# Two transformer blocks on one core: the first feed-forward product and the entry into block two reordered on VectorE and ScalarE

## The reference, cut to what matters

```python
# end of the first block
x = x + m @ w_out
hf = rmsnorm(x, norm_ff_g)
z = relu(hf @ w_ff1)              # 1024 -> 4096
x = x + (z * z) @ w_ff2           # 4096 -> 1024
x = rmsnorm(x, norm_final_g)
# start of the second block
mod = silu(c) @ w_ada + b_ada     # 6 vectors of 1024
shift1, scale1, gate1, shift2, scale2, gate2 = split(mod, 6)
hn = rms_norm(x, g_norm1) * (1 + scale1) + shift1
proj = hn @ w_in                  # q_m k_m v_m o_m gates q_a k_a v_a
# ... mLSTM, attention, w_out, then
x = x + gate2 * hierarchical_moe(...)   # 32 experts, top 2 of one group
return rms_norm(x, g_final)
```

## Time and profile before

| | before |
|---|---|
| median of 3 runs | 1003.87 us (1002.82 to 1003.92) |
| the profiled execution | 1001.12 us |
| its span, first to last instruction | 999.2 us |
| TensorE busy | 971.4 us (97%) |
| VectorE busy | 566.9 us |
| ScalarE busy | 413.9 us |
| granted TensorE clock, mean | 0.997 |
| mean DMA rate | 329 GB/s |

### The profile page before, as it was taken

One profiled execution on the slowest core, in us unless ns is written; L12 is line 12 of the kernel. 1 busy time (PEld: TensorE's weight loads), 2 busy tenths in 40 slices (PEclk: granted clock), 3 DMA queues, 4 the chain that ended last, 5 costly groups with the idle time before them and its releaser, 6 DMA issues.

```text
span 999.2 us, 12464 instructions
## 1 busy us (share of the span) xinstructions
PE 971.4 (97%) x4936; PEld 635.6 (64%) x4936; DVE 566.9 (57%) x880; ACT 413.9 (41%) x647; POOL 83.8 (8%) x72
## 2 busy tenths in 40 slices
PE   8999999999999999989999999999999999899986
PEld 6888888887888888879988534343434343334432
DVE  5677767898989976776986522322323232223222
ACT  7734553445454444666685322222322222122223
POOL 0122003313322030010000000000000000000000
PEclk9999999999999999999999999999999999999999
DMA  9987559986777875545558999999999999999995
GB/s 329 391 306 259 178 170 360 325 292 217 279 255 279 314 270 189 198 159 197 178 198 332 381 417 423 428 429 440 424 439 426 429 433 436 426 425 427 425 424 234
DMA packets 73600, 328.35 MB, mean 329 GB/s; under 512 B 4812, under 2 KB 4976, under 8 KB 61120
## 3 DMA queue, kind: packets, MB, share of 16 engines
q1 hardware_dynamic: 71504, 323.68, 82.6%
q0 software_dynamic: 1888, 3.54, 1.4%
q10 hardware_dynamic: 144, 0.26, 0.1%
HBM read 326.39 MB, written 1.07 MB: 328 GB/s over the span
## 4 chain that ended last, share of the span: by engine, by line
PE 77%; DMA 9%; DVE 8%; ACT 3%; issue 2%; SPq 0%; DVEq 0%; ACTq 0%
PE bank L1095 19%; PE bank L1122 9%; DMA er<-in_w_experts 8%; PE bank L602 6%; PE bank L605 6%; PE bank L599 6%; PE bank L683 4%; PE bank L785 4%; PE bank L1064 3%; DVE wlo L1743 3%; PE bank L687 2%; PE bank L790 2%; PE bank L1134 2%; PE bank L659 2%; PE bank L656 2%
## 5 line engine op out<-in xcount | busy, mean ns | idle before, releaser
L1095 PE MATMUL bank<-er,XT 128*64 128x512 f32 x1024 | 236.1, 600 | 6.6 <-DMA er<-in_w_experts 6.3
L1743 DVE TENSOR_TENSOR wlo<-raw,whi 128x2048 fp32r<-128x2048 f32 x88 | 201.3, 2296 | 68.7 <-ACT whi L1208 68.7
L1208 ACT ACTIVATE whi<-raw 128x2048 fp32r<-128x2048 f32 x88 | 167.0, 1911 | 76.3 <-PE bank L605 33.0
L1095 PEld LDWEIGHTS bank<-er,XT 128*64 128x64 f32 x1024 | 70.4, 137 | 141.6 <-issue 133.7
L1122 PE MATMUL bank<-er,HT 128*64 128x512 f32 x496 | 112.3, 594 | 1.0 <-DMA er<-in_w_experts 1.0
L599 PE MATMUL bank<-whi,hh 128*128 128x512 f32 x224 | 87.9, 393 | 1.4 <-ACT whi L1215 1.4
L602 PE MATMUL bank<-wlo,hh 128*128 128x512 f32 x224 | 87.3, 390 | 0.2 <-DVE wlo L1752 0.2
L605 PE MATMUL bank<-whi,hl 128*128 128x512 f32 x224 | 87.3, 390 | 0.0
L1645 ACT ACTIVATE Y<-bank 64x512 fp32r<-64x512 f32 x62 | 36.6, 591 | 113.9 <-DVE bank L2446 113.1
L683 PE MATMUL bank<-f,whi 128*128 128x512 f32 x224 | 79.4, 399 | 0.0
L1122 PEld LDWEIGHTS bank<-er,HT 128*64 128x64 f32 x496 | 35.1, 137 | 68.4 <-issue 67.5
(11 more groups left out here) (385 smaller groups left out, 1578.1 us busy)
## 6 DMA issues: line engine op xcount, KB each, us to landing
er<-in_w_experts SPq DMA_DIRECT2D x27, 2048.0 KB, 39.4
er<-in_w_experts SPq DMA_DIRECT2D x49, 1024.0 KB, 9.2
er<-in_w_experts SPq DMA_DIRECT2D x12, 4096.0 KB, 34.4
raw<-in_w_in SPq DMA_DIRECT2D x41, 1024.0 KB, 6.2
er<-in_w_experts SPq DMA_DIRECT2D x8, 5120.0 KB, 28.7
raw<-in_w_ff SPq DMA_DIRECT2D x32, 1024.0 KB, 5.8
raw<-in_w_ada SPq DMA_DIRECT2D x24, 1024.0 KB, 5.8
raw<-in_w_out SPq DMA_DIRECT2D x8, 1024.0 KB, 7.3
```

The lines of the kernel that those rows point to most:

```text
L1095: m = e.matmul(b[64 * w:64 * w + 64, :], K.XT[:, j % 5, k, :], K.weights(i)[:, o:o + 512], start=k == 0, stop=k == 7)
L1208: e.activation(whi[K.ring(n)][:, :], raw[h.raw][:, :], ACT.Copy).then_inc(S["hi"], 1)
L1743: e.tensor_tensor(wlo[K.ring(n)][:, :], raw[h.raw][:, :], whi[K.ring(n)][:, :].bitcast(F32), ALU.subtract).then_inc(S["lo"], 1)
```

## The change

- `order_weights`: the `w_ada` half in unit 0 and the second one in unit 1 go; since the list ends after 24, two later ones appear, one in unit 6 and one in unit 7. The weights around them move up or down in the list by one or two places.
- First feed-forward product: VectorE does `x1_out(1)` before `lo(41)`, `f_lo(1)` and the sum of squares before `lo(42)`; ScalarE does `f_hi(1)` before `hi(42)`; TensorE does `turn_f(1)` after chunk 1, not 2.
- Entry: `xg` is split off from `x2_out` (`xg_out`) and, for the last quarter, done five steps later; the last quarter's x is moved ahead of the first `n_lo`; the squares change order with it; `n_lo(0, 7)` goes behind the factor of token block 1. `turn_x2(1, 1)` and `spread(1)` are now done inside token block 0, after chunks 3 and 6. Half 74 is passed on in pieces, the first high piece ahead of ScalarE's copy of the spread factor.
- Later: ScalarE does `hi(85)` before it copies the attention values, not after.

```diff
@@ -24,7 +24,7 @@
 RAW = 6
 RING = 3
 LATE = 96
-PIECED = (0, 1)
+PIECED = (0, 1, 74)
 FIRST2 = 72
 MSC = 128 ** -0.5
 ASC = 64 ** -0.5
@@ -313,10 +313,11 @@
             if g < 8:
                 cols(A["w_ff1"][0], 0, 512 * g)
                 cols(A["w_ff1"][0], 512, 512 * g)
-                ada()
+                if g > 0:
+                    ada()
             if g > 0:
                 rows(A["w_ff2"][0], 512 * (g - 1))
-                if g < 6:
+                if 1 < g < 6:
                     ada()
                 rows(A["w_ff2"][0], 512 * (g - 1) + 256)
         for c0 in (VM, QK, QK + 512, QA, KA, VA, OM):
@@ -614,7 +615,7 @@
             mid()
         dense_half(n + 1, xh, xl, 1, K.at[use], False, True, ready)
 
-    def dense_token(n, xh, xl, t, ready, mid):
+    def dense_token(n, xh, xl, t, ready, between=None):
 
         o = K.at["VM"][t][:, :]
         e.wait_ge(*K.before["VM"][t])
@@ -631,10 +632,10 @@
                 e.matmul(o, a_h, r_l, start=False, stop=False)
                 e.wait_ge(S["x_lo"], ready(k))
                 m = e.matmul(o, a_l, r_h, start=False, stop=k == 7)
-            if t:
-                m.then_inc(S["used"], 1)
-            if hf == 0:
-                mid()
+                if t and c == 3:
+                    m.then_inc(S["used"], 1)
+                if between:
+                    between(k)
 
     def dense_turned(use, n, xh, xl, ready=None, mid=None, each=None):
         free(use)
@@ -791,7 +792,7 @@
         return m
 
     dense_turned("ff0", 40, K.fh, K.fl, (lambda k: SPLIT["f"] + k + 1), None,
-                 lambda k: turn_f(1) if k == 2 else None)
+                 lambda k: turn_f(1) if k == 1 else None)
     for g in range(1, 8):
         dense_paired(f"ff{g}", 38 + 4 * g, K.f2)
         if g == 1:
@@ -825,9 +826,9 @@
 
 
     turn_x2(1, 0)
-    dense_token(72, K.nh, K.nl, 0, (lambda k: SPLIT["n"] + k + 1), lambda: turn_x2(1, 1))
-    spread(1)
-    dense_token(72, K.nh, K.nl, 1, (lambda k: SPLIT["n"] + k + 9), lambda: None)
+    dense_token(72, K.nh, K.nl, 0, (lambda k: SPLIT["n"] + k + 1),
+                lambda k: turn_x2(1, 1) if k == 3 else spread(1) if k == 6 else None)
+    dense_token(72, K.nh, K.nl, 1, (lambda k: SPLIT["n"] + k + 9))
     dense_turned("QK0", 74, K.nh, K.nl)
     free("gates")
     e.wait_ge(S["gw_s"], 4)
@@ -1369,10 +1370,8 @@
         e.wait_ge(S["x"], X_AT["1"] + t + 3)
         e.wait_ge(S["sq"], 5 + t)
         squares(K.x[:, t, 512:1024], 18 + t, K.vjunk[:, 512 * t:512 * t + 512])
+    f_hi(1)
     hi(42)
-
-
-    f_hi(1)
     root(3, 16)
     hi(43)
     for g in range(8):
@@ -1402,13 +1401,13 @@
     def x2_square(t, n):
         i = 2 * t + n
         e.wait_ge(S["x"], X_AT["2"] + i + 1)
-        e.wait_ge(S["sq"], 8 + 2 * i)
+        e.wait_ge(S["sq"], (8, 10, 12, 13)[i])
         squares(K.x[:, t, 512 * n:512 * n + 512], 24 + 4 * n + t, K.junk9[:, 512:1024], EPS ** 0.5 / 32)
 
     def xg_square(t, n):
         i = 2 * t + n
         e.wait_ge(S["xg"], i + 1)
-        e.wait_ge(S["sq"], 9 + 2 * i)
+        e.wait_ge(S["sq"], (9, 11, 14, 15)[i])
         squares(K.xg[:, t, 512 * n:512 * n + 512], 26 + 4 * n + t, K.junk9[:, 0:512], 1.0 / 32)
 
     def x2_root(t):
@@ -1436,18 +1435,20 @@
     x2_square(1, 0)
     e.wait_ge(S["l_col"], 64)
     n_hi(0, (0, 1))
+    x2_square(1, 1)
+    n_hi(0, (2, 3))
     xg_square(1, 0)
-    n_hi(0, (2, 3))
-    x2_square(1, 1)
     n_hi(0, (4,))
     xg_square(1, 1)
     n_hi(0, (5, 6, 7))
     x2_root(1)
+    hi_piece(74, 0)
     spread(1)
     n_hi(1, range(8))
-    hi(74)
+    for c in range(1, 4):
+        hi_piece(74, c)
+    hi(75)
     root(6, 24)
-    hi(75)
     e.wait_ge(S["turned"], TURNED["x2"] + 4)
     e.wait_ge(S["rs"], 6)
     for t in range(2):
@@ -1519,10 +1520,10 @@
             for t, o in ((0, slice(0, 128)), (1, slice(128, 384))):
                 e.activation(Sx[:, hq, o], Sx[:, hq, o], ACT.Exp, bias=stat(k + 4 * t + hq), scale=ASC,
                              accum_out=stat(k + 8 + 4 * t + hq)).then_inc(S["exp"], 1)
+    hi(85)
     e.wait_ge(S["used"], 84)
     for t in range(2):
         e.activation(K.vat[t][:, :], K.at["VA"][t][:, :], ACT.Copy).then_inc(S["vat"], 1)
-    hi(85)
 
     def flat(half):
         return K.PTt[half][:, :, :].rearrange("p h s -> p (h s)")
@@ -1936,16 +1937,16 @@
     x1_out(0)
     lo(40)
     f_lo(0)
+    x1_out(1)
     lo(41)
-    x1_out(1)
-    lo(42)
-
-
     f_lo(1)
     e.wait_ge(S["sq"], 8)
     e.tensor_tensor(stat(16, 2), stat(16, 2), stat(18, 2), ALU.add).then_inc(S["st"], 1)
     e.wait_ge(S["st"], ST_AT["1"] + 1)
-    inv_rms(3, 16, D)
+    e.tensor_scalar(stat(16, 2), stat(16, 2), 1.0 / D, EPS, ALU.mult, ALU.add).then_inc(S["ms"], 1)
+    lo(42)
+    e.wait_ge(S["sd"], 3)
+    e.reciprocal(stat(16, 2), stat(16, 2)).then_inc(S["rs"], 1)
     e.wait_ge(S["rs"], 3)
     e.tensor_tensor(stat(16, 2), stat(16, 2), stat(16, 2), ALU.mult).then_inc(S["st"], 1)
     e.wait_ge(S["l_late"], 16)
@@ -2001,11 +2002,14 @@
             e.wait_ge(S["used"], 72)
         e.scalar_tensor_tensor(out=K.x[:, t, o], in0=K.at["ffo"][i][:, :], scalar=stat(16 + t), in1=K.x[:, t, o],
                                op0=ALU.mult, op1=ALU.add).then_inc(S["x"], 1)
+
+    def xg_out(t, n):
+        o, i = slice(512 * n, 512 * n + 512), 2 * t + n
         e.wait_ge(S["x"], X_AT["2"] + i + 1)
         e.tensor_tensor(K.xg[:, t, o], K.x[:, t, o], K.nfb[:, o], ALU.mult).then_inc(S["xg"], 1)
 
     def x2_sums(t):
-        e.wait_ge(S["sq"], 10 + 4 * t)
+        e.wait_ge(S["sq"], 10 + 5 * t)
         e.scalar_tensor_tensor(out=stat(20 + t), in0=stat(24 + t), scalar=EPS * EPS, in1=stat(26 + t), op0=ALU.add,
                                op1=ALU.add).then_inc(S["st"], 1)
         e.wait_ge(S["st"], ST_AT["2"] + 1 + t)
@@ -2031,25 +2035,29 @@
         e.scalar_tensor_tensor(out=K.nl[:, q, o], in0=K.nf[:, q, o], scalar=K.ada_cols[:, q:q + 1],
                                in1=K.nh[:, q, o].bitcast(F32), op0=ALU.add, op1=ALU.subtract).then_inc(S["x_lo"], 1)
 
-    x2_out(0, 0)
-    x2_out(0, 1)
+    for n in range(2):
+        x2_out(0, n)
+        xg_out(0, n)
     x2_sums(0)
     x2_factor(0)
     x2_out(1, 0)
+    xg_out(1, 0)
     e.wait_ge(S["a1"], 2)
     e.wait_ge(S["ada_rows"], ROWS[10])
     e.wait_ge(S["Rb"], 1)
-    for q in range(3):
-        nf_out(0, q)
+    nf_out(0, 0)
+    nf_out(0, 1)
+    x2_out(1, 1)
     n_lo(0, 0)
-    x2_out(1, 1)
-    for q in range(1, 8):
-        if q < 6:
-            nf_out(0, q + 2)
-        n_lo(0, q)
+    for q in range(1, 7):
+        nf_out(0, q + 1)
+        if q == 3:
+            xg_out(1, 1)
         if q == 6:
             x2_sums(1)
+        n_lo(0, q)
     x2_factor(1)
+    n_lo(0, 7)
     e.wait_ge(S["Rb"], 2)
     nf_out(1, 0)
     nf_out(1, 1)
@@ -2057,10 +2065,11 @@
         if q < 6:
             nf_out(1, q + 2)
         n_lo(1, q)
+    for c in range(4):
+        lo_piece(74, c)
     e.tensor_tensor(stat(24, 2), stat(24, 2), stat(28, 2), ALU.add).then_inc(S["st"], 1)
     e.wait_ge(S["st"], ST_AT["2"] + 3)
     e.tensor_scalar(stat(24, 2), stat(24, 2), 1.0 / EPS, EPS, ALU.mult, ALU.add).then_inc(S["ms"], 1)
-    lo(74)
     e.wait_ge(S["sd"], 6)
     e.reciprocal(stat(24, 2), stat(24, 2)).then_inc(S["rs"], 1)
     for n in range(75, 79):
```

## The result

| | before | after |
|---|---|---|
| median, measured together | 1003.31 us (1002.75 to 1003.92, 6 executions) | 995.65 us (994.58 to 997.51, 6 executions) |
| ratio, 95% interval | | 0.993 (0.992 to 0.994) |
| the profiled execution | 1001.12 us | 997.51 us |
| its span | 999.2 us | 995.6 us |
| granted clock in it, mean | 0.997 | 0.994 |

The change makes the kernel 7.66 us faster. The forecast was 998.4 us with a range from 996.7 to 1001.2: the direction is right, the time lies 1 us under the range. Against 1003.87, the median that the forecast started from, 5.5 us were expected and 8.2 were found.

The account below looks back on a forecast made before the run. TensorE was taken as the bound to 560 us, then TensorE and DMA side by side. Terms 2.35 + 0.3 + 0.1 + 0.85 + 1.45 + 0.5 = 5.55, taken as 5.5, gave 998.4 us from 1003.87; range 996.7 to 1001.2.

Parts of the forecast that it names:

- First product and w_ada halves: First feed-forward product and units 0 and 1: 2.35 us from the new order, 0.3 us from moving the halves.
- the wait at line 687: Unit 1, TensorE waiting for lo(46) behind two w_ada halves: 0.3 us to be saved, 0 as the other end.
- line 656: Chunk 4 of the first feed-forward product: TensorE's 2.19 us wait for f_lo(1) goes, a term of 2.35 us.
- Entry: Entry to block two: token block 0 gives 0.1 us, the spread factor 0.85, half 74 1.45.
- The new wait on `nl`: Token block 0 at the entry: first n_lo begins later behind the last quarter's x, a new stall of 0.5 us.
- Half 74 in pieces: Entry, token block 1: low weights arrive piece by piece, so TensorE's stall at line 659 goes, saving 1.45 us.
- the rival in which the entry gives less back: Block 0 and the factor lose 2 us together, so the gain is 3.5 us: 1000.4 us; chance 0.14.
- OM product: Line 891: hi(85) ahead of the value copies starts 0.53 us earlier, saving 0.5 us, between 0 and 0.6.
- The stream moves: Expert weights from 560 us: DMA stream shifts with TensorE, adding or taking nothing; rival that it stays, 1003 us, chance 0.09.
- the moved sums cost nothing: Unit 7: last two partition sums on GpSimd end before the hand-over is needed, 6 us of cover, cost 0.
- the slower rival: Unit 7: both moved sums fall on the hand-over and hold VectorE, up to 9 us on TensorE: 1007.4 us; chance 0.05.
- The median stands 2.75 us above the profiled execution: Whole kernel: offset added to the forecast profiled execution of 995.6 us, giving a median of 998.4 us.

Follow-up runs that it names:

- only_entry: Kernel before with only the entry part of the change; weight order, first product and hi(85) as before: 1000.72 us, ratio 0.9974.
- busy_first: Kernel before with two unused 128x512 matmuls filling TensorE's stall at line 656: 1002.55 us, ratio 0.9997.
- busy_all: Kernel before with unused matmuls filling the stalls at line 656, before token block 1 and at line 659: 1002.44 us, ratio 0.9997.
- only_first: Kernel before with only the new order of the first feed-forward product, w_ada halves left in place: 1004.48 us, ratio 1.0013.
- only_ada: Kernel before with only the w_ada halves moved, order of the first product as before: 1002.48 us, ratio 0.9991.
- idle7: New kernel with TensorE nearly still at the start of units 1 to 7, eight tiny matmuls waited for one by one: 1030.67 us, ratio 1.0264.
- before_look2: Kernel before, unchanged, profiled and timed once more: 1003.87 us.

## Why the prediction was right, and where it failed

**First product and w_ada halves: 2.65 forecast, 2.98 measured.** VectorE of the new kernel, all 2.2 us late by this execution's start (it turns x at 236.50, before at 234.29):

```profile
243.11 1.28 DVE L1926 TENSOR_TENSOR x<-x,bank 128x512 f32<-128x512 f32 x2 [0.19 <-PE bank L606]
244.31 2.29 DVE L1744 TENSOR_TENSOR wlo<-raw,whi 128x2048 fp32r<-128x2048 f32 x1
247.66 1.66 DVE L1931 SCALAR_TENSOR_TENSOR f<-bank,vec,f 128x256 fp32r<-128x256 f32 x4 [1.06 <-ACT f L1364]
249.23 0.15 DVE L1944 TENSOR_TENSOR st<-st 128x2 f32<-128x2 f32 x1
...
250.19 2.29 DVE L1744 TENSOR_TENSOR wlo<-raw,whi 128x2048 fp32r<-128x2048 f32 x1 [0.60 <-ACT whi L1209]
```

`x1_out(1)`, `lo(41)`, `f_lo(1)`, `lo(42)` follow each other as worked out; less 2.2 us the times are 240.9, 242.1, 245.5 and 248.0, against the 240.9, 242.2, 244.95 and about 247.5 of the forecast. The 0.3 us more are mostly the wait at line 687, which was sized too small. Before, it stands as

```profile
277.72 0.39 PE L683 MATMUL bank<-f,whi 128*128 128x512 f32 x1
278.38 0.39 PE L687 MATMUL bank<-f,wlo 128*128 128x256 f32 x1 [0.27 <-DVE wlo L1743]
```

and counted as the forecast counted line 656, from one start to the next less a step of 0.12 us, it cost 0.54 us, not 0.3. The total held, the split by cause did not: I gave 2.35 us to the order and 0.3 to the halves, as if each could be had alone. The runs of the parts show that the order without the halves is worth nothing, since VectorE's lead in units 0 and 1 is spent on them.

**Entry: 2.4 forecast, 2.55 measured,** and `only_entry` gives the same 2.53. The steps on VectorE, ScalarE and TensorE of the new kernel, each engine's timeline by itself:

```profile
423.12 0.75 DVE L2003 SCALAR_TENSOR_TENSOR x<-bank,st,x 128x512 f32<-128x512 f32 x1 [0.29 <-PE bank L786]
423.79 0.34 DVE L2035 SCALAR_TENSOR_TENSOR nl<-nf,ada_cols,nh 128x128 fp32r<-128x128 f32 x1
...
428.72 0.35 DVE L2023 TENSOR_SCALAR diag<-cst,st 128x128 f32<-128x128 f32 x1
...
434.32 2.49 DVE L1753 TENSOR_TENSOR wlo<-raw,whi 128x512 fp32r<-128x512 f32 x4
```

```profile
428.40 0.61 ACT L1216 ACTIVATE whi<-raw 128x512 fp32r<-128x512 f32 x1
429.75 0.28 ACT L1421 ACTIVATE Rb<-bank 128x128 f32<-128x128 f32 x1 [0.74 <-PE bank L816]
...
433.92 1.66 ACT L1216 ACTIVATE whi<-raw 128x512 fp32r<-128x512 f32 x3
```

```profile
424.18 0.50 PE L634 MATMUL bank<-whi,nl 128*128 128x512 f32 x1 [0.20 <-DVE nl L2035]
...
430.99 0.47 PE L630 MATMUL bank<-whi,nh 128*128 128x512 f32 x1 [0.58 <-ACT nh L1427]
```

The new wait on `nl` is 0.2 us where I had 0.5, the second one of 0.2 did not come, the one at token block 1 is 0.58 where I had 0.7. From the copy of the factor to token block 1 it is 430.99 - 429.75 = 1.24 us, the interval that the forecast carried over from before. Half 74 in pieces leaves no wait at line 660. With these small differences the rival in which the entry gives less back is out.

**OM product: 0.5 forecast, 0.44 measured;** no wait at line 892.

**The stream moves, the moved sums cost nothing.** The sums stand on GpSimd where I put them, ahead of unit 7's hand-over; GpSimd's timeline and VectorE's beside it:

```profile
391.41 5.11 POOL L2630 PARTITION_ALL_REDUCE gate2q<-ada_acc  x1 [50.51 <-DVE ada_acc L1731]
396.43 3.31 POOL L2630 PARTITION_ALL_REDUCE gate2t<-ada_acc  x1
```

```profile
396.52 4.38 DVE L1744 TENSOR_TENSOR wlo<-raw,whi 128x2048 fp32r<-128x2048 f32 x1 [3.09 <-ACT whi L1209]
...
403.59 1.48 DVE L1980 TENSOR_TENSOR zl<-zz,zh 128x512 fp32r<-128x512 f32 x2
```

One VectorE step beside them took 4.38 us in place of 2.29, a sign of the slower rival, and it was covered: the last step of the hand-over begins at 403.59, near the 404.12 of before, and TensorE waits for nothing there. The exclusion that the Trainium skill gives (page "SBUF — State Buffer", section "Who interferes with whom") agrees in kind: the step was held for 2.1 us, though not for the whole of a sum of 5.1 or 3.3 us.

**The step that failed** is the last one of the sum: "The median stands 2.75 us above the profiled execution", carried over as a constant. The sum without it, 1001.1 less 5.5, gives 995.6 us, and the median is 995.65; that is luck, since the stalls gave 5.97 us and the profiled executions of the new kernel took 997.51, 995.87 and 996.16. Three things were wrong in the offset. The first is the median it was taken from: 1003.87, of three executions, where all 151 of the kernel before (alone or beside an experiment) have 1003.19, so that 0.7 us of the 2.75 were chance. The second is what the rest is: the executions of one kernel differ by their granted clock, and the profiled one of before was one with few falls. Executions of both kernels, grouped by the mean clock that each was granted (the 151, and 17 of the new one, on several chips; groups of fewer than four executions are left out):

| mean granted clock | 0.992 | 0.993 | 0.994 | 0.995 | 0.996 | 0.997 |
|---|---|---|---|---|---|---|
| before: mean us (executions) | 1005.05 (13) | 1004.14 (28) | 1003.32 (32) | 1002.60 (54) | 1001.73 (11) | 1001.64 (9) |
| after: mean us (executions) | | | | | 995.54 (7) | 995.85 (4) |

At an equal clock the kernels differ by 6.2 and 5.8 us (standard errors 0.4 and 0.6), which is the size of the 5.97 us of the three stretches, that is of the stalls. One line with a common slope through all the executions gives 6.0 us (0.3). And 0.001 of clock goes with 0.83 us by the table (1005.05 less 1001.73, over four steps), 0.70 by that line. One fall agrees: 3.4 us at half clock (0.66 over 5 us) take 0.0017 off the mean of 1000 us, and cost 1.2 to 1.5. But the mean clock is no pure count of falls that cost. It also holds the fall in the expert stage and the end of the program, after the last matmul; before:

```profile
995.00:999.20 4.20, 0.00 (x0) 0.00 (x0) 0.00 (x0) 0.00 (x0) 0.00 (x0) 0.61 0.62 227
```

The third is that the offset changes with the kernel. The mean clock over the executions is 0.9943 before (without one at 0.944 and 1010.33 us, which stands apart) and 0.9962 after; 1.9 x 0.83 = 1.6 us, or 1.3 with the slope of the line. With the 5.97 that makes 7.3 to 7.6 us, against 7.55 between the pooled medians (1003.19 and 995.64). So the account closes in this form: **6 us of stalls removed, and about 1.5 us of clock that is no longer lost.** And the miss of 2.75 us (998.4 less 995.65) is 0.5 us of stalls more than the 5.5, 0.7 us of a median of three, and the 1.5 of clock.

Of the clock, the fall behind line 656 is shown: 4 of 7 traces at 1.3 us is about 0.75 us an execution. Filling that stall (23 executions of `busy_first` and `busy_all`, against 47 of the kernel before on the same chip) raised the mean clock from 0.9944 to 0.9951 and took 0.6 us off the mean time, with a standard error of 0.3. Where the other 0.6 to 1 us lie stays open. No trace shows a fall behind one of the entry's stalls of 1.3 us, `only_entry` has the mean clock of the kernel before (0.9943) and so gives next to nothing of it, and eighteen traces are too few to place something that happens in half of the executions or less.

The range was too high for the same reason. It took in the bounds of the terms and half a us of scatter of the median, but the offset stood in it as a number without bounds; an offset of 0 as the other end would have put 995.6 us into it. The bounds do not add up as written either: those stated with the terms give a gain from 3.9 to 6.2 us, not 3.5 to 6.8. That did not decide, since the wider pair also ends above the measured time.

## What to carry to other kernels

A profiled execution is one draw: before its offset to the median is carried over, look through its windows for stretches at the lower clock and ask which of them the change touches, since a stall of 2 us in dense TensorE work costs its length and, in about half of the traces here, more than half as much again in clock. When a stall has two engines behind it, moving work on one of them shows next to nothing by itself; the order of VectorE's steps and its load paid only together, so judge such parts as a pair. Compare kernels at an equal granted clock where each execution lists it: here 7.5 us between the medians, with a scatter of 1.4 us between executions, became 6.0 us of stalls, as in the trace.

## What was unexpected of the hardware

- One stand of 2.2 us in otherwise dense work was followed, about 1 us later, by 3.4 us at 1.2 GHz in 4 of 7 traces; a stand of 1.76 us in the one trace of `only_first`, of 1.9 us not in the one of `only_ada`; stands of 3.4 us in 6 of 7 within one execution; stands of 1.3 us at the entry in none of ten traces with two each. The cost was 1.2 to 1.5 us each time. Filled with two matmuls, neither the stand at line 656 (two traces) nor the seven gaps were followed by it.
- Where the stream of weights is a bound beside TensorE, what a fall costs doesn't show. All 18 traces have one between 840 and 890 us, near waits for expert weights; the first window is of the kernel before, the second of `busy_first`, where (as in `only_first`) it is twice as long as elsewhere. The expert stage takes 438.4 us in the one and 438.9 in the other:

```profile
850.00:855.00 5.00, 2.75 (x9) 0.92 (x10) 1.40 (x6) 0.85 (x3) 0.00 (x0) 0.76 0.97 413
```

```profile
860.00:870.00 10.00, 5.48 (x21) 2.62 (x19) 1.16 (x3) 0.35 (x1) 0.00 (x0) 0.66 0.98 423
```

- The fall at 10 to 15 us, at a cost of 1.7 to 2.2 us, came in 3 of 18 traces, of both kernels (after, `idle7`, `before_look2`), with the same code at the start.
